# One decoder step of two layers on one core: a 16-column first tile, rotary halves moved by DMA, and a new order of products where each stage opens

## The chip, the cores and the metric

The kernel runs on one core of a Trainium2 chip. The metric is the device time of one execution in microseconds, the median of several runs: 1350.68 us before the change (three runs, 1350.62 to 1351.5). The execution that the profiler took needed 1351.72 us, and its span from first to last instruction is 1349.6 us.

## The reference

Two layers work on 320 tokens of 1024 features: 256 of a new stream (the prompt) and 64 of a running one (the sample, with 256 past positions). A layer is

```
x += 1/2 * post(SwiGLU_1(pre(x)))                          # ffn, 1024 -> 2*2816 -> 1024
x += post(W_out [GLA | DiffAttn+ALiBi | Retention](pre(x)))  # mixer, W_in: 1024 -> 3344
x += 1/2 * post(SwiGLU_2(pre(x)))
```

with `pre` and `post` RMS norms. What the change touches in the mixer is this:

```
a_lr, gq, gk, gv, gr, dq, dk, dv, rq, rk, rv, rg = jnp.split(z, offs, axis=-1)   # a_lr has 16 columns
log_a = jax.nn.log_sigmoid((a_lr @ P['w_gla_a2'][l] + P['b_gla_a'][l]).astype(jnp.float32)) / GLA_TAU
# _rotary, for each head of 64 columns of rq and rk:
return jnp.concatenate([x1 * cos - x2 * sin, x1 * sin + x2 * cos], axis=-1)
# differential attention, two maps per head:
a = p[:, 0] - lam * p[:, 1]
return jnp.einsum('bhqk,bkhv->bqhv', a, vf)
```

Gated linear attention (GLA) and retention are recurrences evaluated in chunks of 64; the attention has four heads with values of 128 columns. Everything is float32.

## The kernel before, in words

Features lie on the 128 partitions and the 320 tokens along the free dimension, so `x[:, k, :]` is the k-th of 8 blocks of 128 features. A weight tile (a "unit") is 1024 rows by 128 columns: 8 blocks of 128 x 128. Each weight and each activation is split in a high part (`w_h`, `xn_h`: rounded to fp32r) and a low part (`w_l`, `xn_l`: the rest), and one block is multiplied with three matmuls, `w_h xn_l`, `w_l xn_h` and `w_h xn_h` (`product`, L678 to L680), so an ordinary tile is 24 matmuls of 320 columns. SP loads raw tiles into six slots (`load`), ScalarE makes `w_h` (`hi`, L537), VectorE makes `w_l` in place (`lo`, L546), TensorE multiplies, and `w_used` gives the slot back to SP. Matmuls with float32 operands (identity, means, masks, scores) are issued as two instructions each.

Six sub-layers follow each other: ffn1, mixer, ffn2, and again. Between two of them TensorE sums the squares of the output (`stat_y`, L719 and L723), ScalarE takes the root, VectorE the reciprocal (L1414), TensorE spreads it over the partitions (`spread`, L731), and VectorE scales y and adds the first block of it to x; GpSimd adds the others (L554). ScalarE then makes `xn_h` (L1095) and VectorE `xn_l` (L1407), block by block. After `spread`, `keep_busy(6)` (L738) multiplies a constant by the identity six times. The first four tiles of a sub-layer are its opening: for block 0 to 3 TensorE waits for `xn_lo` and does the three products of that block for each of the four tiles (`opening_step`), then each tile's blocks 4 to 7 (`opening`). The statistic of the norm (`stat_x`, L713) is put ahead of the fourth tile. The row scale `rs` (L1447) is applied when a tile leaves PSUM. The first opening of all (`first_opening`) is separate: five warming matmuls of 512 columns (`WARM`, L830), transposes of x as it arrives (`turn_x`, L802), then `first_step(k)` (L816, L819, L822) and the statistic; the tiles 4 and 5 follow in `up_pair(0, 2, False)`.

The mixer is written out by hand in `SCHEDULE`, a list that all engines walk in the same order. ("part", v, k0, k1) are products of input tile v; the rest are steps of the three head groups. Each step marks milestones that others wait for (`mark`, `after`). The GLA scores are made in nine levels: ScalarE exponentiates weights, GpSimd multiplies q and k by them (L583), TensorE multiplies (L915), VectorE copies under a mask (L1587, `score`n). Level n+1 waits for `score`n. `rot` is the rotary step: TensorE multiplies z by a signed permutation (L941) and VectorE does PSUM times sin, z times cos, and the sum (L1646, L1647, L1649). The attention goes through 12 pairs of head and query block: `att_s` (scores, L987 to L991), `att_max`, `att_e`, `att_a` (softmax and difference), `att_t` (transposes of the probabilities, L999; for the sample a product with `fold`, L1001, which adds the two maps), a ScalarE copy, `att_o` (times v, L1012). For the sample's block the 128 rows hold the 64 queries of both maps. Then `squares`, `stat`, `root`, `spread` normalise the heads, and `out` 0 to 7 is the opening of the output projection; its tiles 4 to 7 follow (`U_OUT`). While these run, ScalarE and VectorE evict tile v (`y_tile`, `add_square`) and split the weights of unit 6 + v (v below 5).

## Time and profile before

| | |
|---|---|
| median of three runs | 1350.68 us |
| the profiled execution | 1351.72 us, span 1349.6 us |
| TensorE busy (matmul) | 1330.8 us of the span |
| VectorE, ScalarE, GpSimd busy | 821.7, 637.0 and 132.7 us |
| mean granted TensorE clock | 0.997 of full speed |

The instructions of TensorE overlap: one is drawn from its start until its result has left the array, so its length is more than the distance to the next. Distances from start to start, or the pieces of the chain of waits, tell what an instruction costs. Times are microseconds from the start of the span.

### The profile page before, as it was taken

To read this page: it belongs to the slowest core of one execution; us is meant where nothing else is said; L and a number is where in the kernel's file an instruction comes from.
4 is the path that set the end of the run, shared out by engine and by line. 5 is a ranking of instruction groups with operands and counts; after the bars stand their busy time and mean duration, and the time that the engine had idled before them with its cause. 6 is when DMAs were issued, how large, how long until landed. Compare 5 with 4: busy or idle time off the path is not lost.

```text
span 1349.6 us, 24688 instructions
## 1 busy us (share of the span) xinstructions
PE 1330.8 (99%) x9576; PEld 1300.6 (96%) x9576; DVE 821.7 (61%) x1257; ACT 637.0 (47%) x1011; POOL 132.7 (10%) x153
## 2 busy tenths in 40 slices
PE   8999999999999999999999999999999999999998
PEld 7999999998989999999999999999899999999998
DVE  6755543687766855554386555438876677565532
ACT  5444433654466644443464443437435575444333
POOL 1000000550000200000030000005600030000000
PEclk9999999999999999999999999999999999999999
DMA  7555565543344445555544544555333346555552
GB/s 203 170 168 159 161 167 150 157 128 82 96 119 126 124 143 154 147 141 152 152 121 145 155 144 144 152 152 160 96 96 86 98 125 172 146 149 151 145 144 66
DMA packets 351145, 187.16 MB, mean 139 GB/s; under 512 B 6608, under 2 KB 348396, under 8 KB 351080
## 3 DMA queue, kind: packets, MB, share of 16 engines
q1 hardware_dynamic: 347560, 177.37, 46.6%
q0 software_dynamic: 2736, 8.03, 1.8%
q8 instruction: 45, 0.74, 0.2%
q10 hardware_dynamic: 784, 0.86, 0.2%
q14 instruction: 20, 0.16, 0.0%
HBM read 181.90 MB, written 4.33 MB: 138 GB/s over the span
## 4 chain that ended last, share of the span: by engine, by line
PE 92%; DVE 4%; DVEq 1%; issue 1%; ACT 1%; DMA 1%; POOL 0%; ACTq 0%; SPq 0%; POOLq 0%
PE ps L678 28%; PE ps L679 27%; PE ps L680 27%; DVE w_l L546 1%; PE ps L987 1%; PE ps L915 1%; PE ps L738 1%; PE ps L890 1%; PE ps L1012 1%; PE ps L830 1%; PE ps L1025 1%; PE ps L731 0%; PE ps L1001 0%; PE ps L723 0%; DVE tiny L1623 0%
## 5 line engine op out<-in xcount | busy, mean ns | idle before, releaser
L678 PE MATMUL ps<-xn_l,w_h 128*128 128x320 f32 x1808 | 569.7, 315 | 1.2 <-DVE xn_l L1407 0.8
L679 PE MATMUL ps<-xn_h,w_l 128*128 128x320 f32 x1808 | 558.5, 309 | 0.0
L680 PE MATMUL ps<-xn_h,w_h 128*128 128x320 f32 x1808 | 558.4, 309 | 0.0
L546 DVE TENSOR_TENSOR w_l<-raw,w_h 128x1024 fp32r<-128x1024 f32 (+1 forms) x338 | 407.5, 1209 | 167.2 <-ACT w_h L537 166.7
L537 ACT ACTIVATE w_h<-raw 128x1024 fp32r<-128x1024 f32 (+1 forms) x338 | 348.4, 1035 | 216.5 <-DMA raw<-in_ffn_w_down_dram 124.9
L678 PEld LDWEIGHTS ps<-xn_l,w_h 128*128 128x128 f32 x1808 | 339.8, 188 | 6.8 <-DVE xn_l L1407 2.0
L679 PEld LDWEIGHTS ps<-xn_h,w_l 128*128 128x128 f32 x1808 | 339.9, 188 | 1.7
L680 PEld LDWEIGHTS ps<-xn_h,w_h 128*128 128x128 f32 x1808 | 339.7, 188 | 0.0
L678 PE MATMUL ps<-hid_l,w_h 128*128 128x320 f32 x704 | 217.5, 309 | 0.0
L680 PE MATMUL ps<-hid_h,w_h 128*128 128x320 f32 x704 | 217.4, 309 | 0.0
L679 PE MATMUL ps<-hid_h,w_l 128*128 128x320 f32 x704 | 217.4, 309 | 0.0
L679 PEld LDWEIGHTS ps<-hid_h,w_l 128*128 128x128 f32 x704 | 132.2, 188 | 0.0
L680 PEld LDWEIGHTS ps<-hid_h,w_h 128*128 128x128 f32 x704 | 132.2, 188 | 0.0
L678 PEld LDWEIGHTS ps<-hid_l,w_h 128*128 128x128 f32 x704 | 132.2, 188 | 0.0
L1486 DVE TENSOR_TENSOR gate<-ps,rs 128x320 f32<-128x320 f32 x72 | 35.3, 490 | 157.7 <-PE ps L680 157.5
L1153 ACT ACTIVATE gate<-gate 128x320 f32<-128x320 f32 x72 | 34.0, 472 | 146.6 <-DVE gate L1486 146.5
L554 POOL TENSOR_TENSOR x<-x,y 128x320 f32<-128x320 f32 x35 | 36.9, 1087 | 330.2 <-DVE y L1418 330.2
L1157 ACT ACTIVATE hid_h<-up 128x320 f32 (+1 forms) x72 | 34.0, 473 | 70.8 <-DVE up L1492 70.8
L1138 ACT ACTIVATE sq<-ps 128x320 f32<-128x320 f32 x48 | 20.8, 434 | 48.6 <-PE ps L680 48.5
L1492 DVE TENSOR_TENSOR up<-up,gate 128x320 f32<-128x320 f32 x72 | 35.5, 492 | 12.4 <-issue 11.4
L1260 ACT ACTIVATE probs<-probs,tiny 128x128 f32<-128x128 f32 (+2 forms) x40 | 19.3, 482 | 47.9 <-DVE tiny L1623 47.9
L678 PE MATMUL ps<-xw_l,w_h 128*128 128x320 f32 x128 | 40.1, 313 | 0.0
(270 smaller groups left out, 1208.3 us busy)
## 6 DMA issues: line engine op xcount, KB each, us to landing
raw<-in_ffn_w_up_dram SPq DMA_DIRECT2D x172, 512.0 KB, 3.8
raw<-in_ffn_w_down_dram SPq DMA_DIRECT2D x64, 448.0 KB, 3.7
raw<-in_w_in_dram SPq DMA_DIRECT2D x54, 512.0 KB, 3.8
raw<-in_ffn_w_down_dram SPq DMA_DIRECT2D x32, 512.0 KB, 3.9
raw<-in_w_out_dram SPq DMA_DIRECT2D x16, 512.0 KB, 4.1
const<-in_tables_dram POOLq DMA_DIRECT2D x8, 298.0 KB, 4.4
raw<-in_ffn_w_up_dram SPq DMA_DIRECT2D x8, 256.0 KB, 6.4
x_in<-in_x_prompt_dram SPq DMA_DIRECT2D x4, 256.0 KB, 6.2
```

The lines of the kernel that those rows point to most:

```text
L537: act.activation(w_h[s][:, 0:cols], raw[s][:, 0:cols], ACT.Copy).then_inc(w_hi, 1)
L546: dve.tensor_tensor(w_l[s][:, 0:cols], raw[s][:, 0:cols], w_h[s][:, 0:cols], ALU.subtract).then_inc(w_lo, 1)
L554: pool.tensor_tensor(x[:, k, :], x[:, k, :], y[:, k, :], ALU.add).then_inc(x_new, 1)
L678: pe.matmul(out, w_h[s][:, w], xl, start=first, stop=False)
L679: pe.matmul(out, w_l[s][:, w], xh, start=False, stop=False)
L680: return pe.matmul(out, w_h[s][:, w], xh, start=False, stop=last)
L1138: act.activation(sq[b][:, :], ps[:, bank, 0:T], ACT.Square).then_inc(y_sq, 1)
L1153: act.activation(gate[q][:, :], gate[q][:, :], ACT.Silu).then_inc(silu, 1)
L1157: act.activation(tile(hid_h, v), up[q][:, :], ACT.Copy).then_inc(hid_hi, 1)
L1260: i = act.activation(p, p, ACT.Exp, bias=tiny[:, 8 + 2 * s + m:9 + 2 * s + m], accum_out=tiny[:, 12 + 2 * s + m:13 + 2 * s + m])
L1486: dve.tensor_tensor(gate[q][:, :], ps[:, 2 * q, 0:T], rs[:, :], ALU.mult).then_inc(up_mul, 1)
L1492: dve.tensor_tensor(up[q][:, :], up[q][:, :], gate[q][:, :], ALU.mult).then_inc(prod, 1)
```

## The change

In words, in the order of a layer:

- `first_opening`: three warming matmuls of 320 columns where there were five of 512, and the first piece of x_sample comes by SP's queue, ahead of the first weights, not by ScalarE's. The tiles 4 and 5 come into this function: their `w_h xn_h` and `w_h xn_l` products go first, then the wait for `w_lo` and the `w_l xn_h` products; `stat_x` and the transposition of the parameters stand within tile 4. ScalarE makes the high part of unit 4 one step earlier.
- `opening_step`: per block first `w_h xn_h` of four tiles, then `w_l xn_h` of four, and only then the wait for `xn_lo` and `w_h xn_l` of four. It waits for `xn_hi` and for the low parts of all four tiles at its start.
- `spread`: one matmul of 256 constant columns is put ahead of its wait; `keep_busy` makes 4 in place of 6.
- The first tile of the mixer holds 16 columns: its high part lies in columns 0 to 15 of each block and its low part in columns 32 to 47, so that two products per block do for three, and `a2` is loaded twice. Load, `hi` and `lo` of this tile are 16 columns wide.
- `rot` loses its matmul. SP exchanges the halves of rq and rk with eight DMAs per layer (SBUF to SBUF, 32 partitions each), queued among the weight loads behind a wait for `evac`; sin carries the sign. The four VectorE steps move in `SCHEDULE` from before levels 0 and 1 and after levels 2 and 3 to after levels 1, 2, 3 and 4.
- `att_t` of the sample's block is three transposes; `att_o` multiplies 128 columns for it, and VectorE adds the two maps' halves after ScalarE's copy (`att_o`, milestone of DVE), for which `squares` waits.
- While the output tiles run, the weights ahead are split after tiles 3 to 6 (`AHEAD_OUT`), not after tiles 0 to 4 and 6.

```diff
+AHEAD_OUT = {3: (6,), 4: (7, 8), 5: (9, 10), 6: (11,)}
-WARM = 5
+WARM = 3
 SCHEDULE = (
...
-    ... tile_steps(6) + [("past", 0), ("past", 1), ("rot", 0), ("weight", 0)]
-    + P8[7][:1] + [("rot", 1), ("weight", 1)] + P8[7][1:]
+    ... tile_steps(6) + [("past", 0), ("past", 1), ("weight", 0)]
+    + P8[7][:1] + [("weight", 1)] + P8[7][1:]
...
+   ("level", 1), ("rot", 0), ... ("level", 2), ("rot", 1), ... ("level", 3), ("rot", 2), ... ("level", 4), ("rot", 3),
...
+    add("sin", np.sin(ang.astype(np.float32)) * np.where(r % 64 < 32, -1.0, 1.0)[:, None])
 # SP
+                if k == 0:
+                    sp.dma_start(x_in[64:128, 2, 0:2 * P], ins["x_sample"][0, :, 0:2 * P]).then_inc(x_chunk[0], 16)
+                sp.dma_start(low_rank(raw[slot(l, U_MIX)], 0), columns(ins["w_in"], l, slice(0, RANK))
+                             ).then_inc(raw_in[slot(l, U_MIX)], 16)
+                for v in range(1, N_MIX):
...
+                    n = v - RQ - 8
+                    if n in (0, 2):
+                        sp.wait_ge(evac, l * GROUPS + G_MIX + RQ + n + 3)
+                        for g in range(0, P, 32):
+                            sp.dma_start(y[g:g + 32, n:n + 2, :], z[g ^ 32:(g ^ 32) + 32, RQ + n:RQ + n + 2, :]
+                                         ).then_inc(turned_halves[n // 2], 16)
 # TensorE
+            def low_rank_part(s, bank, k0, k1):
+                for k in range(k0, k1):
+                    w = w_h[s][:, k * P:(k + 1) * P]
+                    pe.matmul(ps[:, bank, 0:T], w, xn_l[:, k, :], start=k == 0, stop=False)
+                    mm = pe.matmul(ps[:, bank, 0:T], w, xn_h[:, k, :], start=False, stop=k == KD - 1)
...
             def opening_step(l, u0, n, i, order=range(KD), xh=xn_h, xl=xn_l):
+                pe.wait_ge(w_lo, l * UNITS + u0 + OPENING)
+                pe.wait_ge(xn_hi, (l * 4 + n) * KD + i + 1)
+                for t in range(OPENING):
+                    pe.matmul(out(t), block(w_h, t), xh[:, k, :], start=i == 0, stop=False)
+                for t in range(OPENING):
+                    if u0 + t != U_MIX:
+                        pe.matmul(out(t), block(w_l, t), xh[:, k, :], start=False, stop=False)
                 pe.wait_ge(xn_lo, (l * 4 + n) * KD + i + 1)
                 for t in range(OPENING):
-                    if i == 0:
-                        pe.wait_ge(w_lo, l * UNITS + u0 + t + 1)
-                    tile_part(slot(l, u0 + t), t, i, i + 1, order, xh, xl)
+                    mm = pe.matmul(out(t), block(w_h, t), xl[:, k, :], start=False, stop=i == KD - 1)
...
             def spread(l, m):
+                pe.matmul(ps_rs[:, 0:256], C("ident"), const[:, 0:256], start=True, stop=True)
                 pe.wait_ge(inv_out, l * 3 + m + 1)
...
-                    keep_busy(6)
+                    keep_busy(4)
...
+                for t in range(OPENING, OPENING + 2):      # first_opening
...
+                    part(w_h[t], xn_h, 0, KD, first=True)
+                    part(w_h[t], xn_l, 0, KD)
+                    pe.wait_ge(w_lo, t + 1)
+                    if t == OPENING:
+                        part(w_l[t], xn_h, 0, KD // 2)
+                        pe.wait_ge(first_consts, 16)
+                        stat_x(0, 0)
+                        part(w_l[t], xn_h, KD // 2, KD, last=True).then_inc(w_used, 1)
...
                     for kt in range(KEYS[ATT[n][1]]):      # att_t
-                            mm = pe.matmul(ps[:, 6, kt * P:kt * P + T_S], p, C("fold"), start=True, stop=True)
+                        mm = pe.transpose(ps[:, 6, kt * P:(kt + 1) * P], p, C("ident"))
 # VectorE
+                elif kind == "att_o":
+                    if n % 3 == 2:
+                        after(dve, l, "act", f"att_o{n}")
+                        v = y[:, 2 + n // 3, T_P:T]
+                        mark("dve", dve.tensor_tensor(v, v, ps[:, 7, T:T + T_S], ALU.add), f"att_o{n}")
                 elif kind == "rot":
-                    zt, t = z[:, RQ + n, :], y[:, 7, :]
-                    after(dve, l, "pe", f"rot{n}")
-                    dve.drain()
-                    dve.tensor_tensor(t, ps[:, ROT_BANK[n], 0:T], C("sin"), ALU.mult)
+                    zt, t = z[:, RQ + n, :], y[:, n, :]
+                    dve.wait_ge(turned_halves[n // 2], (l + 1) * 64)
+                    dve.tensor_tensor(t, t, C("sin"), ALU.mult)
                     dve.tensor_tensor(zt, zt, C("cos"), ALU.mult)
```

## Rows read from the trace of the kernel before

**Rows 1.** The page: busy time, share and instructions of each engine.
```profile
PE 1330.8 (99%) x9576; PEld 1300.6 (96%) x9576; DVE 821.7 (61%) x1257; ACT 637.0 (47%) x1011; POOL 132.7 (10%) x153
```

**Rows 2.** Chain of waits: start, length, engine and line, instructions merged.
```profile
280.82 0.54 PE ps L941 x2
...
281.51 0.15 PE ps L679
...
308.48 0.33 PE ps L890 x3
...
351.35 0.61 PE ps L1001 x6
```

**Rows 3.** Timeline, ffn1 to mixer, layer 0: start, length, then idle and releaser.
```profile
250.95 2.76 PE L738 MATMUL ps<-const 128*128 128x256 f32 x12
...
252.25 0.56 ACT L1095 ACTIVATE xn_h<-x,par 128x320 fp32r<-128x320 f32 x1 [0.82 <-DVE x L1424]
...
253.97 0.41 PE L678 MATMUL ps<-xn_l,w_h 128*128 128x320 f32 x1 [0.26 <-DVE xn_l L1407]
```

**Rows 4.** Timeline, mixer to ffn2, layer 0.
```profile
435.21 0.93 PE L731 MATMUL ps<-const,inv 128*128 128x128 f32 x6 [0.47 <-DVE inv L1414]
...
437.38 0.56 ACT L1095 ACTIVATE xn_h<-x,par 128x320 fp32r<-128x320 f32 x1 [2.42 <-DVE x L1424]
...
440.08 0.50 PE L678 MATMUL ps<-xn_l,w_h 128*128 128x320 f32 x1
...
445.74 0.81 DVE L1407 SCALAR_TENSOR_TENSOR xn_l<-x,par,xn_h 128x320 fp32r<-128x320 f32 x1 [0.28 <-ACT xn_h L1095]
```

**Rows 5.** Busy time of stretches; the eighth entry, after POOL, is the granted clock.
```profile
248.70:252.10 3.40, 2.93 (x20) 2.66 (x21) 1.04 (x3) 2.20 (x5) 1.44 (x2) 1.00 0.79 228
...
436.50:439.80 3.30, 3.30 (x9) 2.60 (x8) 3.21 (x7) 1.58 (x4) 2.06 (x3) 0.50 0.03 10
675.40:678.70 3.30, 3.30 (x11) 2.94 (x12) 1.70 (x5) 0.56 (x1) 0.24 (x1) 0.50 0.38 113
```

**Rows 6.** Timeline of the beginning.
```profile
10.23 0.83 PE L816 MATMUL ps<-xn_h,w_h 128*128 128x320 f32 x4 [0.39 <-ACT xn_h L1095]
...
12.04 2.65 SPq L484 DMA_DIRECT2D const<-in_tables_dram  x1
...
28.26 0.78 PE L713 MATMUL ps<-ssum,const 128*128 128x320 f32 x2 [2.06 <-DVE ssum L1442]
```

**Rows 7.** Timeline of VectorE and TensorE: what tile 6 waits for.
```profile
34.33 2.35 DVE L546 TENSOR_TENSOR w_l<-raw,w_h 128x1024 fp32r<-128x1024 f32 x2
...
36.82 0.41 PE L678 MATMUL ps<-xn_l,w_h 128*128 128x320 f32 x1 [0.20 <-DVE w_l L546]
```

**Rows 8.** Line L478 in the window 2.0 to 3.2: x's second piece.
```profile
L478 SPq DMA_DIRECT2D x_in<-in_x_prompt_dram x1: 602/602/602, 2.7 to 2.7; - x1
...
DMA to landing us min/median/max: 6.0/6.0/6.0
```

**Rows 9.** VectorE's groups from 289 to 306.2: busy, mean ns, idle before.
```profile
L1587 DVE COPY_PREDICATED probs<-mask,ps 128x384 f32<-128x384 uint8 x3 | 1.8, 587 | 2.1 <-PE ps L915 1.7 <-issue 0.2 <-PE ps L890 0.2
L1649 DVE TENSOR_TENSOR z<-z,y 128x320 f32<-128x320 f32 x2 | 1.7, 851 | 0.1
L1647 DVE TENSOR_TENSOR z<-z,const 128x320 f32<-128x320 f32 x2 | 1.3, 648 | 0.0
L1646 DVE TENSOR_TENSOR y<-ps,const 128x320 f32<-128x320 f32 x2 | 1.0, 492 | 0.2
```

**Rows 10.** Timeline of the levels, of both engines.
```profile
305.38 0.70 PE L915 MATMUL ps<-sq 32*64 32x64 f32 x40 [0.99 <-DVE probs L1587]
...
306.23 0.58 DVE L1587 COPY_PREDICATED probs<-mask,ps 128x384 f32<-128x384 uint8 x1 [1.00 <-PE ps L915]
```

**Rows 11.** Timeline of TensorE, end of the heads and of the output tiles.
```profile
404.47 0.83 PE L1029 MATMUL ps<-const,z 128*128 128x1 f32 x6 [0.35 <-ACT z L1283]
...
433.24 0.74 PEld L719 LDWEIGHTS ps<-const,ssum 128*128 128x128 f32 x6 [0.30 <-DVE ssum L1478]
```

More of the change, by code:

```diff
@@ L164, in milestones @@
                 act.append(f"att_o{n}")
+                dve.append(f"att_o{n}")
         elif kind == "squares":
@@ L204, in constants @@
     add("head128", np.ones((P, 1)) / 128.0)
-    rot = np.zeros((P, P))
-    for g in (0, 64):
-        for i in range(32):
-            rot[g + 32 + i, g + i] = -1.0
-            rot[g + i, g + 32 + i] = 1.0
-    add("rot", rot)
     pos = np.concatenate([np.arange(T_P), PAST + np.arange(T_S)]).astype(np.float32)
@@ L215, in constants @@
     add("cos", np.cos(ang.astype(np.float32)))
-    add("sin", np.sin(ang.astype(np.float32)))
+    add("sin", np.sin(ang.astype(np.float32)) * np.where(r % 64 < 32, -1.0, 1.0)[:, None])
     lg = np.log(1.0 - 2.0 ** (-5.0 - np.arange(H)))
@@ L274, in build @@
         NCONST = sum(n for _, n in table_at.values())
-        FIRST = table_at["rot"][0]
+        FIRST = table_at["cos"][0]
         N_PAR = 16 * 9
@@ L394, in build @@
         masks_loaded = sem("masks_loaded")
+        turned_halves = [sem(f"rotary_halves_exchanged{n}") for n in range(2)]
         par_mm = sem("par_mm")
@@ L829, in first_opening @@
                 for _ in range(WARM):
-                    pe.matmul(ps[:, 3, :], sq_2[:, 0:P], sq_2[:, P:P + 512], start=True, stop=True)
+                    pe.matmul(ps[:, 3, 0:T], sq[0][:, 0:P], sq[0], start=True, stop=True)
                 pe.wait_ge(pads_set, 2)
@@ L841, in first_opening, with part @@
                         turn_x(k + 3)
-                pe.wait_ge(first_consts, 16)
-                stat_x(0, 0)
-                pe.wait_ge(par_loaded, N_PAR)
-                pe.transpose(ps_m[:, 3, 0:ROWS], par_in[0:ROWS, :], C("ident")[0:ROWS, 0:ROWS]).then_inc(par_mm, 1)
+                for t in range(OPENING, OPENING + 2):
+                    def part(w, v, k0, k1, first=False, last=False):
+                        for k in range(k0, k1):
+                            mm = pe.matmul(ps[:, t, 0:T], w[:, k * P:(k + 1) * P], v[:, k, :], start=first and k == 0,
+                                           stop=last and k == KD - 1)
+                        return mm
+                    pe.wait_ge(w_hi, t + 1)
+                    part(w_h[t], xn_h, 0, KD, first=True)
[6 more added lines that the diff above has]
+                        part(w_l[t], xn_h, KD // 2, KD, last=True).then_inc(w_used, 1)
+                        pe.wait_ge(par_loaded, N_PAR)
+                        pe.transpose(ps_m[:, 3, 0:ROWS], par_in[0:ROWS, :], C("ident")[0:ROWS, 0:ROWS]).then_inc(par_mm, 1)
+                    else:
+                        part(w_l[t], xn_h, 0, KD, last=True).then_inc(w_used, 1)
             half_rows = lambda h: slice(64 * (h % 2), 64 * (h % 2) + 64)
@@ L933, in mixer_step @@
                     mark("pe", heads_out(5 + n, n, scores, gv_tok, s0_a, q_s[:, :]), f"gla_o{n}")
-                elif kind == "rot":
-                    pe.wait_ge(evac, l * GROUPS + G_MIX + RQ + n + 2)
-                    if n >= 2:
-                        shared_free(l, kind, n)
-                    else:
-                        after(pe, l, "act", "abs")
-                        after(pe, l, "dve", "minus")
-                    mark("pe", pe.matmul(ps[:, ROT_BANK[n], 0:T], C("rot"), z[:, RQ + n, :], start=True, stop=True), f"rot{n}")
                 elif kind == "ret_s":
@@ L1071, in _ @@
                 spread(l, 1)
-                keep_busy(6)
+                keep_busy(4)
                 ffn(l, U_F2, G_F2, 4, 3, 2)
@@ L1082, in _ @@
             act.dma_start(par_in[0:DEPTH * KD, :], ins["ffn1_norm_pre"].rearrange("l (k p) -> (l k) p", p=P)).then_inc(gain_loaded, 16)
-            for c in range(KD // 2):
+            for c in range(1, KD // 2):
                 cols = slice(2 * c * P, 2 * (c + 1) * P)
@@ L1124, in pre @@
                     split_hi(l, n, k, x, norm)
+                    if l == 0 and n == 0 and k == KD - 1:
+                        hi(act, l, u0 + 4)
                     if k:
@@ L1127, in pre @@
                 square(KD - 1)
-                for v in (4, 5):
+                for v in (5,) if l == 0 and n == 0 else (4, 5):
                     hi(act, l, u0 + v)
```

80 lines of the change are left out of this document (45 added, 35 removed).

## The prediction

> **What bounds the kernel now.** I read the page first: TensorE is busy for 1330.8 of 1349.6 us [rows 1]. Nothing near 10% can be had without taking matmuls away, and nearly every matmul that goes is time. But VectorE, at 821.7 us, is not far behind on average, and in some stretches it decides; so I went to the chain of waits for the price of one matmul, and to the timelines of the places that the diff touches for what is late there. In the chain a product of 320 columns takes 0.15 us (0.1465 over long stretches), a float32 matmul of 320 columns such as `rot` 0.54 for its two instructions, the three `fold` matmuls 0.61, three transposes 0.33 [rows 2]. The timelines show TensorE idle, or occupied with constants, at three kinds of place: each passage between sub-layers [rows 3, 4], the beginning [rows 6, 7], and VectorE's chain in the GLA levels [rows 10].
>
> The profiled execution took 1351.72 us, 1.04 above the median. I work out a difference against it and take it from the median, 1350.68.
>
> **Passages (five).** In ffn1 to mixer, `keep_busy` fills 250.95 to 253.71 and the first product starts at 253.97, released by `xn_lo`. `xn_hi` of block 0 is there at 252.25 + 0.56 = 252.81 [rows 3]. After the change four constant matmuls, 2.76 x 4/6 = 1.84, end at 252.79, and products start at 252.8: 1.1 us earlier. The eight products that need no `xn_lo` take 1.17, about what it still lacks. The matmul added to `spread` stands in the wait for the reciprocal, 0.47 us by the idle time of L731 [rows 4]; for 256 columns it takes 0.54 x 256/320 = 0.43 [rows 2]. So it costs nothing while that wait covers it, and at half the clock at most 0.43.
>
> From the mixer to ffn2 the same step was worse: `keep_busy` ran at clock 0.50 [rows 5], so products started only at 440.08, while `xn_hi` was there at 437.94 [rows 4]. The granted clock fell to its lower level (1.2 GHz) in two stretches, here and at 675.4, while after ffn1 of layer 0, where less of the stretch was idle, it stayed at 1.00 (2.4 GHz) [rows 5]. The filler in `spread` adds work exactly there; I take it that the clock holds. Then products start at 437.95, 2.1 us earlier. The next limit is `xn_lo` of block 7, at 446.55 [rows 4]: tile 0 needs it after 4 x 12 + 9 products (8.35 us), at 446.3, so almost nothing is lost. In the mixer's passages it is lost a little sooner, because the first tile has fewer products. Sum outside the mixer's own start: 2.1 + 2.1 (the one at 675) + 1.1 (mixer to ffn2 of layer 1, as in rows 3) = 5.3. If the clock falls all the same, each of the first two gives 1.4 less: lower bound 2.5.
>
> **The mixer, per layer.** TensorE loses 1.1 at the passage, 8 products of the first tile (1.17; most of it swallowed by the wait for `xn_lo` of block 7), and four `rot` matmuls, 4 x 0.54 = 2.16 [rows 2]. If TensorE decided alone, that would be 3.3 to 4.4. It doesn't. Level n+1 waits for `score`n, VectorE does the rotary steps between them, and TensorE stands idle for 0.99 at level 5 already [rows 10]. Before, two of four rotary steps were over when the levels began; now all four lie between score 1 and score 5. One costs 0.49 + 0.65 + 0.85 = 2.0 us, so two more are 4.0. The product with sin read PSUM; now both its inputs are in SBUF, like those of the other two products, which take 0.65 and 0.85 where L1646 takes 0.49 [rows 9]: 0.16 to 0.36 more each, about 1.0 for four. VectorE's spare time in this stretch is 2.1 and the 1.00 ahead of score 5 [rows 9, 10], 3.1. It starts earlier by what TensorE gained until level 1, 1.1 + 2 x 0.54 = 2.2. What arrives at level 5 and 6 is 2.2 + 3.1 - 4.0 - 1.0 = 0.3. So I cost the rotary part at a gain of 0.3 per layer, the passage and the narrow tile included. Bounds: 3.3 if VectorE's waits give way, -1.0 if the four steps cost 2.3 each and the spare time can't be used.
>
> The Trainium skill speaks to this too (SBUF — State Buffer, "SBUF: two separate sides"): a VectorE operation with two SBUF inputs and a GpSimd operation that reads SBUF lock each other out for a whole instruction. By that rule the sin product can wait out a GpSimd multiplication; the trace agrees for the two products that it could concern, and by the rule in full the gain of 0.3 would be a loss.
>
> The eight rotary DMAs stand in SP's queue. They wait for tile 6's and tile 8's eviction, well before the next weight load is due (a tile is 24 products, 3.5 us). An issue took between 0.6 [rows 8] and 2.65 us [rows 6]; I take 0.6, the form being plain, so four fit and nothing is late. The narrow tile makes load, `hi` and `lo` shorter; nobody waits for them, so 0.
>
> Fold: 0.61 becomes 0.33 four times a layer [rows 2], 1.1. The trace has no `att_o` of the sample's block at 128 columns. From below it costs what it did, from above its six instructions take 6 x 0.54/2 x 128/320 = 0.65 where six of 64 columns take 0.61, as the fold's [rows 2]; I take the upper end, 0.04 x 4 lost. The last block adds VectorE's addition ahead of `squares` c, for which TensorE already stands 0.35 [rows 11]: between 0.1 and 0.5, I take 0.3. Net 0.6.
>
> Output tiles: TensorE (its weight load) waits 0.30 for VectorE's last addition of squares, behind a weight split of 1.2 [rows 11, 7]; with the split put behind it, 0.2 is gained. The splits of tiles 6 and 7 come later, but TensorE works on tiles 4 and 5 for 7 us; if that cover failed, each would cost up to 1 us.
>
> Per layer 0.3 + 0.6 + 0.2 = 1.1, two layers 2.2, with bounds of -0.4 and 8.2.
>
> **The beginning.** TensorE idles 2.06 before `stat_x` [rows 6], and now tile 4 starts there. But tile 6 waits for its low part, which ended at 36.68, not for TensorE [rows 7], and VectorE makes that only after `rs`, which hangs on `stat_x`. That statistic now comes 20 products, 2.93 us, after the opening's last, where it came 2.2 after (the idle 2.06 and the last product's 0.15): 0.7 later. The start itself: `turn_x(2)` stands ahead of the first step and needs x's second piece, which landed at 2.65 + 6.0 = 8.6 [rows 8], now issued some 0.6 later. The first step thus comes at 9.0 to 9.6, not at 10.23 [rows 6]: 0.6 to 1.2 gained. Together -0.1 to 0.5 gained, and with a lower clock, for TensorE has less to do before 9 us, about 1.5 lost. I take 0.
>
> **Sum.** 5.3 + 2.2 + 0 = 7.5: 1344.2 for the profiled execution, 1343.2 for the median.
>
> **Rivals.**
> A. *TensorE decides everywhere.* Each removed matmul is time, the rotary steps fit. For it: 1330.8 us of TensorE [rows 1]. Against it: 0.99 idle at level 5 [rows 10]. Per layer 3.3 instead of 0.3: 6.0 more, 1337.2.
> B. *The clock falls more often.* Shorter warming, four constants for six, and a first stretch in which only three transposes per block run. For it: two of five passages fell already [rows 5]. Against it: the filler. It costs 1.5 at the beginning and 1.4 at two passages: 1347.5. The Trainium skill (TensorE: Matmul & The Clock Gate, Part 4) says that transposes don't count as busy for the clock as other matmuls do; no row here tests it. By it this rival is likelier at the beginning, where transposes take the place of the warming.
> C. *Slower.* The SP queue holds the weights back: if each rotary issue takes 2.65 us [rows 6], four take 10.6, 7.1 beyond the tile that covers them, and ScalarE, which walks one list, stands at the weight's high part with the level weights behind it. Four such groups are up to 28 us: 1371. It turns the forecast's gain into a loss from (7.5/4 + 3.5)/4 = 1.3 us per issue on.
> D. *The rotary steps wait for their DMAs or lock with GpSimd,* each 0.5 dearer: 4.0 lost, 1347.2.
>
> **How the numbers follow.** Forecast 0.46 (own range 1341 to 1345), A 0.23, B 0.14, D 0.11, C 0.04, and 0.02 for a loss from some other new wait. The range 1337.3 to 1347.6 holds the first four but for their tails. Within 0.2% (2.7 us, about what a measurement can tell from no change) begins at 1348: the tails of B and D, 0.04. Slower is C and the other loss, 0.06, and faster 0.90.
>
> **What would show it.** No `fold` or `rot` in TensorE's groups; the first product of a passage right after `xn_hi` and `keep_busy`; clock 1.00 at the passages; a wait of TensorE on L1587 at levels 4 to 7 of 1 to 3 us a layer, where A has none; L713 of the beginning near 28; SP's rotary issues at 0.6. I am wrong if TensorE's waits in the levels are below 0.5 (A), or if ScalarE waits for a weight right after the rotary DMAs (C).

## The result, and the profile after

The changed kernel takes 1355.16 us (median of 13 runs, 1349.92 to 1357.66) where the kernel before takes 1350.6 beside it: ratio 1.0033, 95% interval 1.0026 to 1.004. It is slower, by 4.6 us or 0.33%; I had forecast 1343.2. The profiled execution is itself one of 1355.16 us, with a span of 1353.4. Over the 13 runs the time goes largely with the mean granted clock: the fastest, 1349.92, had 0.998, the four slowest (1355.98 to 1357.66) 0.992 or 0.993.

The page's row of busy times answers to [rows 1]: TensorE lost 8.2 us of work, and the span grew by 3.8.

```profile
PE 1322.6 (98%) x9506; PEld 1294.2 (96%) x9506; DVE 822.2 (61%) x1265; ACT 636.9 (47%) x1011; POOL 135.9 (10%) x153
```

Where the time went can be read from the starts of the same TensorE instructions in both traces. In the table, a positive number is time lost against the kernel before within that stretch. The third column is the changed kernel with the old beginning (the first experiment), where only the rest of the change acts.

| stretch (start before, us) | forecast | changed | old beginning |
|---|---|---|---|
| start to first `spread` (250.18) | 0 | +5.05 | +0.35 |
| layer 0, first `spread` to level 8 (315.11) | -0.3 | -0.15 | +0.13 |
| layer 0, level 8 to `spread` after the output tiles (435.21) | -0.8 | +1.74 | +1.45 |
| layer 0 mixer to ffn2, and ffn2 (673.12) | -2.1 | -1.33 | -1.88 |
| ffn2 to ffn1 of layer 1 (675.28 to 913.16) | -2.1 | -1.84 | -1.86 |
| layer 1, first `spread` (915.26) to level 8 | -0.3 | +0.23 | 0.00 |
| layer 1, level 8 to `spread` (1100.11) | -0.8 | +0.74 | +0.79 |
| layer 1 mixer to ffn2, and ffn2 (1339.49) | -1.1 | -0.72 | -0.73 |

(Stretches leave out the wait for the reciprocal in ffn passages, which differs by up to 0.11. The +0.23 holds a fall of the clock at 970.2.) Three things failed: the beginning, the part from the heads to the last output tile, and a little of the passages. The beginning alone turns the sign.

**Beginning.** The timeline of TensorE, then of VectorE; columns are start, length, engine and line, then idle time and releaser. The last two rows are the end of tile 5 and the start of tile 6, which started at 36.82 before [rows 7].

```profile
5.83 0.55 PE L844 MATMUL ps<-const,x_in 128*128 128x128 f32 x3
9.50 0.90 PE L844 MATMUL ps<-const,x_in 128*128 128x128 f32 x3 [3.12 <-DMA x_in<-in_x_prompt_dram]
10.05 1.41 PE L858 MATMUL ps<-xn_h,w_h 128*128 128x320 f32 x4
...
30.81 0.70 PE L754 MATMUL ps<-ssum,const 128*128 128x320 f32 x2
...
34.39 1.34 PE L887 MATMUL ps<-xn_h,w_l 128*128 128x320 f32 x8
39.30 0.63 PE L697 MATMUL ps<-xn_l,w_h 128*128 128x320 f32 x1 [3.57 <-DVE w_l L565]
```
```profile
32.02 2.15 DVE L1492 RECIPROCAL rs<-sq 128x320 f32<-128x320 f32 x1 [0.86 <-ACT sq L1145]
...
36.81 2.35 DVE L565 TENSOR_TENSOR w_l<-raw,w_h 128x1024 fp32r<-128x1024 f32 x2
```

The first step starts at 10.05 (before: 10.23), but four products take 1.41 where they took 0.83 [rows 6], and the last product of the eight steps starts 1.84 late (27.73 against 25.89). `stat_x` is 2.55 late (30.81 against 28.26): 1.84 by those steps, the other 0.71 because it now stands behind 20 products. `rs` and the low part of tile 6 hang on it, and tile 6 starts 2.48 late. TensorE, which had done the tiles 4 and 5 by then, stands idle for 3.57 ahead of it. The remaining 2.57 are lost between there and the first `spread`. The view of the granted clock (the last figure but two in each row) shows a slow stretch for each half of the loss:

```profile
0.00:7.60 7.60, 4.43 (x13) 2.60 (x13) 2.30 (x5) 1.28 (x1) 1.41 (x6) 1.00 0.59 175
7.60:14.40 6.80, 4.90 (x20) 4.86 (x21) 2.83 (x6) 4.46 (x9) 0.00 (x0) 0.50 1.11 348
14.40:38.30 23.90, 21.33 (x147) 20.87 (x145) 20.19 (x37) 14.45 (x23) 3.43 (x3) 1.00 0.63 165
38.30:45.20 6.90, 5.90 (x22) 5.91 (x23) 5.64 (x11) 3.74 (x7) 0.00 (x0) 0.51 0.29 69
441.10:444.50 3.40, 3.40 (x13) 2.88 (x13) 1.21 (x4) 0.17 (x1) 0.00 (x0) 0.50 0.31 92
675.40:678.80 3.40, 3.40 (x26) 3.40 (x26) 1.18 (x1) 2.25 (x2) 0.00 (x0) 1.00 0.56 167
970.20:973.60 3.40, 3.40 (x15) 3.40 (x14) 3.20 (x4) 0.00 (x0) 1.68 (x1) 0.50 0.07 17
```

Twice, 6.8 to 6.9 us at 1.2 GHz. The first time TensorE had done no more than a few transposes in the 3.0 us since its warming ended, the second time it had been idle for 2.6. The drop that [rows 5] show at 675.4 is gone; the one at 436.5 has moved to 441.1.

**Levels.** TensorE waits for VectorE at three levels of layer 0, the levels 3, 4 and 5 (one before, 0.99 [rows 10]); in layer 1 it waits twice, 1.14 and 1.54. VectorE's groups from 289 to 311.5 give the price of a rotary step, 0.83 + 0.62 + 0.80 = 2.25.

```profile
301.00 0.70 PE L972 MATMUL ps<-sq 32*64 32x64 f32 x40 [0.98 <-DVE probs L1632]
...
305.63 0.70 PE L972 MATMUL ps<-qk 32*64 32x64 f32 x40 [1.53 <-DVE probs L1632]
...
310.28 0.70 PE L972 MATMUL ps<-sq 32*64 32x64 f32 x40 [1.22 <-DVE probs L1632]
```
```profile
L1695 DVE TENSOR_TENSOR y<-y,const 128x320 f32<-128x320 f32 x4 | 3.3, 827 | 0.0
L1698 DVE TENSOR_TENSOR z<-z,y 128x320 f32<-128x320 f32 x4 | 3.2, 797 | 0.3
L1696 DVE TENSOR_TENSOR z<-z,const 128x320 f32<-128x320 f32 x4 | 2.5, 615 | 0.0
```

**Output tiles.** The first step of output tile 0, TensorE's timeline: it stands 1.10 for VectorE's low parts, a wait the kernel before did not have. The statistic of the last heads waits 0.61 (before: 0.35 [rows 11]). `stat_y` starts 1.04 later than the usual distance from one product to the next; before it was 0.20. From start to start the pieces are: level 8 to the statistic of the first heads 83.31 (before 83.89), from there to output tile 0 2.78 (1.77), to the statistic of the last heads 3.95 (3.69), to `stat_y` 29.56 (28.78). In layer 1 the first three are the same within 0.03, and the fourth is as before (28.58 against 28.56).

```profile
404.50 0.49 PE L1047 MATMUL ps<-const,probs 128*128 128x128 f32 x3
406.10 0.83 PE L726 MATMUL ps<-xw_h,w_h 128*128 128x320 f32 x4 [1.10 <-DVE w_l L565]
...
410.05 0.83 PE L1074 MATMUL ps<-const,z 128*128 128x1 f32 x6 [0.61 <-ACT z L1330]
...
439.61 0.83 PE L760 MATMUL ps<-const,ssum 128*128 128x1 f32 x6 [0.87 <-DVE ssum L1523]
```

**Passages.** ffn1 to mixer, layer 0, answers to [rows 3]: `keep_busy` is 1.89 long, not 2.76, and the first product follows it directly.

```profile
255.99 1.89 PE L780 MATMUL ps<-const 128*128 128x256 f32 x8
258.01 0.83 PE L726 MATMUL ps<-xn_h,w_h 128*128 128x320 f32 x4
```

### The profile page after: what moved, and what is told of

It reads as the page before. It is cut to its first block, busy times and chain, and to the rows that moved or that the text cites. A ratio compares the mean times of both kernels' runs of the same rounds, so it can differ in the third digit from the quotient of the medians.

```text
span 1353.4 us, 24588 instructions
## 1 busy us (share of the span) xinstructions
PE 1322.6 (98%) x9506; PEld 1294.2 (96%) x9506; DVE 822.2 (61%) x1265; ACT 636.9 (47%) x1011; POOL 135.9 (10%) x153
## 4 chain that ended last, share of the span: by engine, by line
PE 89%; DVE 5%; POOL 2%; DMA 1%; DVEq 1%; issue 1%; ACT 1%; SPq 0%; ACTq 0%; POOLq 0%
PE ps L697 26%; PE ps L699 26%; PE ps L698 26%; POOL x L573 2%; DVE w_l L565 1%; PE ps L726 1%; PE ps L732 1%; PE ps L729 1%; DMA raw<-in_ffn_w_up_dram 1%; PE ps L948 1%; PE ps L972 1%; PE ps L1036 1%; PE ps L1070 1%; PE ps L1057 0%; DMA x_in<-in_x_prompt_dram 0%
## 5 line engine op out<-in xcount | busy, mean ns | idle before, releaser
L697 PE MATMUL ps<-xn_l,w_h 128*128 128x320 f32 x1704 | 537.3, 315 | 3.6 <-DVE w_l L565 3.6
L698 PE MATMUL ps<-xn_h,w_l 128*128 128x320 f32 x1704 | 528.0, 310 | 0.0
L699 PE MATMUL ps<-xn_h,w_h 128*128 128x320 f32 x1704 | 527.9, 310 | 0.0
L697 PEld LDWEIGHTS ps<-xn_l,w_h 128*128 128x128 f32 x1704 | 321.7, 189 | 7.7 <-issue 4.8
L698 PEld LDWEIGHTS ps<-xn_h,w_l 128*128 128x128 f32 x1704 | 321.8, 189 | 1.0
L699 PEld LDWEIGHTS ps<-xn_h,w_h 128*128 128x128 f32 x1704 | 321.7, 189 | 0.0
L1140 ACT ACTIVATE xn_h<-x,par 128x320 fp32r<-128x320 f32 x48 | 27.0, 563 | 25.1 <-DVE x L1469 11.2
```

The costliest lines, as they stand in the source:

```text
L697: pe.matmul(out, w_h[s][:, w], xl, start=first, stop=False)
L698: pe.matmul(out, w_l[s][:, w], xh, start=False, stop=False)
L699: return pe.matmul(out, w_h[s][:, w], xh, start=False, stop=last)
L1140: act.activation(dst[:, k, :], src[:, k, :], ACT.Copy, scale=scale).then_inc(xn_hi, 1)
```

## The experiments

Theory: the beginning costs about 5, by a low clock in the first steps and by `stat_x` behind 20 products. The rest gains only 1 to 2, for the rotary steps lie in VectorE's level chain and the first output tile waits for four low parts at once. Main rival: the beginning is no cause, and time comes back elsewhere as the clock moves. Each kernel was timed with 11 runs unless said. Times of the kernel before beside them: 1350.5 to 1350.6. The edits are given in short.

### The old beginning

```diff
-WARM = 3   (320 columns)      +WARM = 5   (512 columns)
-x_sample piece 0 by SP        +all four pieces by ACT
-tiles 4, 5 around stat_x      +stat_x, then up_pair(0, 2)
```

> The changed kernel with the beginning of the kernel before: five warming matmuls of 512 columns, all four pieces of x_sample issued by ACT, tiles 4 and 5 of the first FFN by up_pair behind stat_x, hi(4) behind the squares. Everything else is as changed. Theory 'the beginning': the first spread of the changed kernel starts 5.05 us later than before (255.22 against 250.18), the rest of the change is worth -1.3 in all (the end is +3.7), so this kernel ends 5 under the changed one: 1350 (1348.5 to 1351.5), first spread at 250.2, tile 6 at 36.8. Rival 'the clock moves elsewhere': a beginning without its extra half-speed windows lets one fall at a later passage (spread of the mixer, 435 or 1100), and only 1.5 to 3.5 of the 5 come back: 1352 to 1353.5. Rival 'something behind the beginning': the first spread was late for another reason, the time stays within 1 of 1355.

Measured: 1350.04 (1349.42 to 1352.01), ratio 0.9997, interval 0.9988 to 1.0006. That is 5.1 under the changed kernel, and the first `spread` is at 250.53. The theory holds: without the new beginning the kernel is as fast as the one before, and the rest of the change brings nothing that the time can show. Of the 5.5 us between the two profiled executions 4.7 lie ahead of the first `spread`; the other 0.8 lie behind it, mostly where the clock of the changed kernel fell, at 441.1 and 970.2, and this one's did not. So a part of the rival stands: the clock falls at different places (here at 28.9 and 302.0), and whether the beginning has to do with the later falls is not shown.

### Its three parts, each undone alone on the changed kernel

```diff
 e5_warm:  +WARM = 5, 512 columns
 e6_tiles: +stat_x behind the eight steps, tiles 4, 5 by up_pair
 e9_x:     +x_sample piece 0 by ACT
```

> The changed kernel with one part undone: the five warming matmuls of 512 columns instead of three of 320. The old beginning as a whole gave back 5.1. Theory 'warming': in the changed kernel the clock is at 0.50 from 7.6 to 14.4, over the first step and a half, which puts stat_x 2.5 later (30.8 against 28.3), and all that follows (rs, the low parts of tile 6, the idle 3.9 ahead of tile 6, the second window at half clock from 38.3) comes from that: with the old warming the first step runs at 1.00, the second window goes, and the time is 1350 to 1351, -4 to -5. Rival 'order of tiles 4 and 5': the idle time ahead of tile 6 comes from stat_x standing behind 20 products: the old warming then gives back only the 2 of the first window, 1353. Rival 'the piece of x': turn_x(2) still waits for the x piece that lands at 9.45, behind a warming that ends near 8; only 1 comes back.

> The changed kernel with one part undone: tiles 4 and 5 of the first FFN by up_pair behind stat_x, stat_x right behind the eight first steps, hi(4) behind the squares. Warming and the order of the x pieces stay as changed. Theory 'order of tiles 4 and 5': stat_x comes 20 products (2.9 us) earlier, rs and the low parts of tile 6 with it; TensorE has tiles 4 and 5 (7 us) to cover them, the idle 3.9 ahead of tile 6 falls to some 1 and the second window at half clock goes: first spread 3 to 3.5 earlier, 1351.5 to 1352. Rival 'warming': the order of tiles 4 and 5 is what it saves, not what it costs, and the time stays at 1355 or rises by up to 1, the idle time then standing ahead of stat_x (2.06 in the kernel before).

> The changed kernel with one part undone: all four pieces of x_sample are issued by ACT, none by SP between the first x piece and the first weights. Theory 'SP late': in the changed kernel the first raw weights land at 7.82 against 6.03 and the second x piece at 9.45, and turn_x(2) stands 3.12 for it; with one issue less ahead of them on SP (0.6 to 0.7 each) these land some 1 earlier, the first step starts 1 to 2 earlier (8 to 9), still at half clock: 1353 to 1354, and if TensorE's idle stretch shrinks enough for the clock to stay up, 1351. Rival 'ACT late instead': the sample piece is late on ACT and turn_x(0) waits for it; no gain, within 0.7 of 1355.

Measured: warming 1351.63 (1351.12 to 1354.2), tiles 1351.55 (1350.11 to 1353.81), piece of x 1352.98 (1350.11 to 1355.14). The three sum to 9.3 where all together gave 5.1. One reason is that they share a loss. The other is the clock behind the beginning: in the profiled executions the three are at the first `spread` only 2.5, 2.6 and 1.1 ahead of the changed kernel, and the other 0.7 to 1.1 of each lies behind it, where none of the three profiles has the falls at 441.1 and 970.2. Views of the granted clock and the waits show how the loss is shared. With the old warming the eight steps run at full clock and take 15.69 from the first product to the last (before 15.66, changed 17.68). The idle time ahead of tile 6 stays all the same, and a slow stretch follows it:

```profile
7.60:14.40 6.80, 6.42 (x40) 5.24 (x39) 4.92 (x11) 4.50 (x11) 0.00 (x0) 1.00 1.09 344
38.00:41.40 3.40, 3.40 (x13) 3.40 (x14) 2.81 (x5) 1.89 (x3) 0.00 (x0) 0.50 0.20 50
```
```profile
37.94 0.58 PE L697 MATMUL ps<-xn_l,w_h 128*128 128x320 f32 x1 [3.56 <-DVE w_l L565]
```

With the old order of tiles 4 and 5 the first steps stay slow (their first four products take 1.42), but the wait of 3.57 at tile 6 is gone, against the old idle 2.07 ahead of `stat_x`. Tile 6 starts no earlier for it (39.47 against 39.30); what is saved is the slow stretch behind it, for the only slow stretch behind `stat_x` (30.9 to 34.3) falls on the tiles 4 and 5:

```profile
29.74 0.78 PE L754 MATMUL ps<-ssum,const 128*128 128x320 f32 x2 [2.07 <-DVE ssum L1469]
30.79 0.55 PE L697 MATMUL ps<-xn_l,w_h 128*128 128x320 f32 x1 [0.17 <-DVE w_l L565]
```

Without SP's extra issue the wait for x's piece is 1.92, not 3.12, but the first step starts only 0.37 earlier (9.68) and stays at 0.50. `stat_x` (30.94) and tile 6 start no earlier than in the changed kernel:

```profile
39.42 0.63 PE L695 MATMUL ps<-xn_l,w_h 128*128 128x320 f32 x1 [3.56 <-DVE w_l L563]
```

The 1.1 at its first `spread` is a second slow stretch half as long in this profile (39.1 to 42.5); that the piece of x is the cause is not shown. So my theory on the warming was too strong (3.5, not 4 to 5): the idle time of 3.57 is there at full clock too and comes from the order of the tiles alone. Filling 2.06 of idle time opened one of 3.57, which costs as much as the warming does.

### Rotary halves by the constant matmul again

```diff
-("level", 1), ("rot", 0) ... ("level", 4), ("rot", 3)
+("past", 1), ("rot", 0) ... ("rot", 1), ("weight", 1) ... ("level", 2), ("rot", 2) ... ("level", 3), ("rot", 3)
-dve.wait_ge(turned_halves[n // 2], (l + 1) * 64)
+after(dve, l, "pe", f"rot{n}")
```

> As the kernel with the old beginning, and the rotary halves come from the constant matmul again, at the four old places of SCHEDULE (two before level 0, two behind levels 2 and 3), with no exchange by DMA. Theory 'DVE pays for the rotary': with the exchange the levels gave back 1.8 in layer 0 and 2.2 in layer 1 while the two matmuls removed before level 0 gained 1.05 and 1.08, so the matmul form is 0.7 to 1.1 faster per layer, 1.5 to 2 in all: 1348 to 1348.5 if the old beginning alone gives 1350; TensorE starts levels 4 to 8 without the waits of 1.1 to 1.7 us on L1587. Rival 'TensorE pays': four 384-column matmuls less are 4 x 0.54 per layer of TensorE's time, so the matmul form is 1 to 2 slower per layer (+2 to +4 against the old beginning alone). Rival 'no matter': the level waits come from other edits (AHEAD_OUT, low-rank tile), within 0.5.

Measured: 1349.26 (1347.3 to 1349.99), 0.8 under the old beginning alone, with intervals that overlap. The traces say it more sharply. Counted from the first `spread` of each layer, against the kernel before, the exchange is 1.5 and 1.1 ahead of the matmul form at level 0, loses 2.07 and 1.95 from level 2 to level 8, where the matmul form loses nothing, and is 0.54 and 0.89 behind it there. (The clock fell at 302 in the kernel with the exchange; in the changed kernel, where it did not, the 2.07 are 1.79. The expectation calls the matmuls 384 columns wide; they have 320.)

### The low parts of the output tiles waited for later

```diff
-pe.wait_ge(w_lo, l * UNITS + u0 + OPENING)
+pe.wait_ge(w_hi, l * UNITS + u0 + OPENING)
 pe.wait_ge(xn_hi, ...)
 for t in range(OPENING): w_h * xh
+pe.wait_ge(w_lo, l * UNITS + u0 + OPENING)
 for t in range(OPENING): w_l * xh
```

> As the kernel with the old beginning, and opening_step waits for the high parts of its four tiles ahead of the first products and for the low parts only behind the four w_h x xh products. Theory 'output tiles wait for all low parts': the first step of the output tiles stood for 1.10 in layer 0 and 1.29 in layer 1 on w_l of all four tiles; it now starts about 1 earlier in each, and what is late next is the squares of the third group of heads (0.61): 1.0 to 2.2 less than the old beginning alone, 1348 to 1349. Rival 'the low parts are late anyway': the wait only moves four products (about 0.7 us) down, and the gain is 0.7 per layer less what the following wait takes, under 0.5 in all. The same edit touches the opening tiles of the FFN and of the mixer, where the low parts are already there: no change there.

Measured: 1348.55 (1347.84 to 1351.99), 1.5 under the old beginning alone, with intervals that overlap; the traces give 0.86 and 0.90 from level 8 to the output tiles' end in the two layers. The wait of 1.10 shrinks to 0.28, behind four products (TensorE's timeline):

```profile
400.63 0.85 PE L724 MATMUL ps<-xw_h,w_h 128*128 128x320 f32 x4
401.76 0.86 PE L728 MATMUL ps<-xw_h,w_l 128*128 128x320 f32 x4 [0.28 <-DVE w_l L563]
```

The theory holds in size and place: a loop over four tiles that had waited tile by tile now waited for the last of four.

### The old places of the weight splits

```diff
-AHEAD_OUT = {3: (6,), 4: (7, 8), 5: (9, 10), 6: (11,)}
+AHEAD_OUT = {0: (6,), 1: (7,), 2: (8,), 3: (9,), 4: (10,), 6: (11,)}
```

> As the kernel with the old beginning, and AHEAD_OUT spreads the high splits of output tiles 6 to 11 as before (one per evicted tile, from tile 0 on). Theory 'late splits': in the changed kernel stat_y of the mixer stood 0.7 to 1.0 in layer 0 behind an ACT that waited for the raw weights (1.67 and 0.70 idle at 433.08 and 436.65); with the old places the last output tiles start 0.5 to 1 earlier in layer 0 and not at all in layer 1: 0.5 to 1 less, 1349 to 1349.5. Rival 'the places don't matter': the raw weights land when they land, and ACT waits there in either order, within 0.3 of the old beginning alone. Rival 'the change was right': splits at tiles 0 to 2 delay the evictions of those tiles, 0.3 to 1 slower.

Measured: 1351.57 (1350.76 to 1353.46), 1.5 slower. My theory fell: the later splits are no loss. With the old places `stat_y` of layer 0 starts 1.65 later than a product's usual distance, with the new ones 1.01; in layer 1 0.68 against 0.14. Part of the 1.5 is the clock, which fell at 438 and 1066 in the profiled run: the piece around 1066 took 1.55 more.

### Rotary steps late, and early

Both on the kernel with the old beginning and the later wait (1348.55).

```diff
 e8_rotlate:   +("level", 5), ("rot", 0) ... ("level", 8), ("rot", 3)
 e10_rotearly: +P8[7][:1], ("rot", 0) ... ("part", 8, 0, 5), ("rot", 1) ... level 2, rot 2 ... level 3, rot 3
```

> As the kernel with the old beginning and the later wait for low parts (1348.55), and the four rotary steps with their exchange by DMA stand behind levels 5, 6, 7 and 8 in SCHEDULE, not behind 1 to 4. In the kernel with the old beginning TensorE stood at levels 3 to 5 of layer 0 for 1.14 and 1.70 on VectorE, whose step behind level 1 took 1.85 + 1.00 + 1.71 beside GpSimd at 290.8 to 295.4 and 0.48 x 3 once GpSimd was idle. Theory 'place, not exchange': behind level 5 GpSimd is idle and VectorE has 2.5 us of gaps; the levels keep 1 to 1.6 of the 2.07 they gave back in layer 0 and about 1 of 0.9 to 1 in layer 1: 1346 to 1347. Rival 'VectorE is full either way': 4 x 1.45 us more between level 5 and ret_dec make the retention decays late, ret_kt waits 2 to 3 per layer: 1348 to 1351. Rival 'no matter': within 0.5 of 1348.5.

> As the kernel with the old beginning and the later wait for low parts (1348.55), with the exchange by DMA and the rotary steps nearly where the matmul form has them: 0 and 1 ahead of level 0 (behind tile 7's first half and tile 8's first part), 2 and 3 behind levels 2 and 3. The first exchange lands at 283.6, so step 0 can run from there. VectorE is idle 1.7 + 1.1 us between 282 and 288.3, and a step takes 1.45 alone and up to 4.6 beside GpSimd. With the steps behind levels 5 to 8 levels 3 to 5 kept their gain (-3.8 at level 5) but gave back 2.4 by level 8 and 1.5 more by the heads. Theory 'place': two steps in the idle time ahead of level 0 cost level 0 at most 1, and the levels give back at most 1 in place of 2.07: 1347 to 1348. Rival 'VectorE has a fixed sum of work from 276 to 317': whatever the place, levels plus heads come out within 0.5 of 1348.5. Rival 'beside GpSimd it is dearest': two steps of 3 to 4.6 us there make tile 7's and 8's evictions late, TensorE stands 2 ahead of level 0: 1350 to 1352.

Measured: late 1348.25 (1347.61 to 1349.37), early 1356.33 (5 runs, 1353.79 to 1356.95). Late, levels 3 to 5 kept what was won (level 5 at -3.81 against the kernel before), then levels 7 and 8 gave back 2.4 and the stretch from there to the heads, where `ret_kt` needs VectorE's decays, 1.7. What is left is 0.3 in the time, less than these runs can tell from nothing: the work is VectorE's, wherever it stands. Early, it stands for the exchange itself. VectorE's timeline of that kernel:

```profile
281.12 1.23 DVE L563 TENSOR_TENSOR w_l<-raw,w_h 128x1024 fp32r<-128x1024 f32 x1
285.40 0.82 DVE L1676 TENSOR_TENSOR y<-y,const 128x320 f32<-128x320 f32 x1 [3.05 <-DMA y<-z]
286.14 1.02 DVE L1677 TENSOR_TENSOR z<-z,const 128x320 f32<-128x320 f32 x1
287.24 1.72 DVE L1679 TENSOR_TENSOR z<-z,y 128x320 f32<-128x320 f32 x1
```

TensorE then stands 3.44 ahead of level 1. I had expected the exchange to have landed at 283.6, when its last DMA had been issued; here a DMA of it lands 2.0 to 2.6 after its issue. The only idle time that VectorE has ends before the halves are there; that is what the matmul form could use.

### Without the filler in `spread`

```diff
-pe.matmul(ps_rs[:, 0:256], C("ident"), const[:, 0:256], start=True, stop=True)
```

> As the kernel with the old beginning (1350.04), without the one 256-column product that spread makes ahead of its wait for inv. Theory 'the filler holds the clock': the kernel before fell to 0.50 at 436.4 and 675.4, in two of the five passages; the changed kernel with the old beginning held 1.00 at all of them. Without the filler the clock falls again at one or two passages, 1.7 us each: 1351.5 to 1353. Rival 'the order of the products fills the passage': opening_step now begins with four products of high parts while the low part of x is made; TensorE's idle time in the passage is shorter by that and not by the filler: within 0.5 of 1350. Rival 'the filler is in the way': 0.1 each of five passages, 1349.5.

Measured: 1351.39 (1349.81 to 1352.53), 1.35 above the old beginning alone, with intervals that overlap. The clock falls at both passages again, where with the filler the same windows show 1.00:

```profile
437.30:440.70 3.40, 3.40 (x12) 2.95 (x12) 2.10 (x5) 0.56 (x1) 0.64 (x1) 0.50 0.08 24
676.20:679.60 3.40, 3.40 (x11) 3.04 (x12) 1.63 (x4) 0.56 (x1) 0.17 (x1) 0.51 0.38 110
```
```profile
437.30:440.70 3.40, 3.20 (x19) 2.68 (x20) 2.49 (x5) 0.69 (x2) 1.03 (x2) 1.00 0.09 28
675.40:678.80 3.40, 3.28 (x19) 2.72 (x19) 2.30 (x5) 0.56 (x1) 0.84 (x2) 1.00 0.37 110
```

It doesn't hold it always: of twelve profiled kernels with the filler the clock fell near 436 to 441 in four, near 675 in none; of two without it (this one and the kernel before), in both at both places.

### The fold matmuls back

```diff
-pe.transpose(..., C("ident")) for the sample's block, 128 columns, VectorE adds the halves
+pe.matmul(..., C("fold")), 64 columns, no addition
```

> As the kernel with the old beginning and the later wait for low parts (1348.55), with the constant fold matmuls of the attention heads back (and the narrow eviction, and no addition on VectorE behind every third head). I forecast 0.6 per mixer for their removal; the traces show 0.24 between level 8 and the statistic of the heads in each mixer, and 0.26 lost again at the statistic of the last heads, which waits for ACT's squares behind VectorE's addition (0.78 against 0.52 before). Theory 'a wash': back with the fold, within 0.4 of 1348.5. Rival 'forecast right, hidden elsewhere': the removal gives 0.6 per mixer, 1349.8. Rival 'the addition costs more': without it the time is 0.5 to 1 lower, 1347.6 to 1348.

Measured: 1348.55 (1347.4 to 1349.91), the same. A wash in the time, but not in the traces. From level 8 to the statistic of the first heads it takes 83.91 in both layers, where every kernel with the transposes but the one with the late rotary steps takes 83.30 to 83.57: the transposes gain about 0.6 a layer there, not the 0.24 that I wrote ahead of the run. VectorE's addition takes 0.26 back, for with the fold the statistic of the last heads waits 0.35 again:

```profile
405.16 0.83 PE L1061 MATMUL ps<-const,z 128*128 128x1 f32 x6 [0.35 <-ACT z L1315]
```

That leaves some 0.33 a layer for the transposes, 0.7 in all, which is within what the times of two such kernels differ by chance.

### What has shown a gain, together

```diff
 old beginning, rotary by matmul, later wait for the low parts; passages, filler, AHEAD_OUT and transposes as changed
```

> The kernel with the old beginning, the rotary halves by the constant matmul at the old places (1349.26 with that alone), and the wait for the low parts behind the first products (1348.55 with that alone). If the two add up: 1350.04 - 0.8 - 1.5 = 1347.75 (1347 to 1348.3). Rival 'one hides the other': the passage that each shortens ends in the same wait (squares of the third group of heads) and only one counts, 1348.5. It is also the kernel that keeps of the change only what has shown a gain: passages, high parts first, the transposes in place of the fold.

Measured: 1346.69 (1345.98 to 1348.6), ratio 0.9975, interval 0.9966 to 0.9984. It beats both kernels: 3.8 under the one before, beside which it ran, and 8.5 under the changed one's median. The rotary matmuls were worth 1.9 here and 0.8 without the later wait; the ranges overlap, so the difference of the two is not shown.

Three parts of the change were never undone alone: the narrow first tile, the order of products within `opening_step`, and four constants for six.

## Why the prediction was wrong

- **The beginning, forecast 0, was +5.05.** This is the step that failed most, and it failed in three places. First, my own terms did not give 0: at most 0.5 gained against 1.5 lost by the clock is a loss of 1.0 to 1.6. Second, the gain by an earlier start was 0.18, not 0.6 to 1.2, and the low clock cost 2.02 in the eight steps, not 1.5; with the 0.71 of the statistic, which I had right as 0.7, that makes `stat_x` 2.55 and tile 6 2.48 late. Third, I put the idle time ahead of tile 6 at nothing. I had written that tile 6 hangs on `rs` and not on TensorE, and so had the idle time (3.57) before me, but not what follows it: a second stretch at half clock, 6.9 us long, for another 2.57. The experiments part the two: with the old warming the steps are at full speed and the idle time stays (3.56), with the old order of tiles it goes.
- **Rival B** named this mechanism ("less to do before 9 us") and priced it at 1.5 there, a third of what it was; it did not have the second stretch. The clock at 0.50 from 7.6 on stands behind a stretch with a few transposes in it. By the Trainium skill (TensorE: Matmul & The Clock Gate, Part 4) transposes don't count as busy in the same way. That agrees, but TensorE was also idle there, and no run here parts the two.
- **Rotary, passage into the mixer and narrow tile, forecast 0.3 a layer,** was 0.15 gained in layer 0 and 0.23 lost in layer 1, the latter with a fall of the clock; the other profiles with this form and place, where they have no fall there, show between 0.17 gained and 0.09 lost. The mechanism was right: four steps in the level chain, at 2.25 on average where I had 2.0 + 0.25. That the average fits is in part luck: the first step took 4.56 beside GpSimd, the other three 1.46 each. The waits of TensorE at the levels (3.7 in layer 0, 2.7 in layer 1) are about the 1 to 3 that I named, at the levels 3 to 5 where I had 4 to 7. Rival A, TensorE decides, fell. (Its 1337.2 lies just outside the range that was to hold it.)
- **Rule on the shared side of SBUF.** The step at 290.81 in the kernel with the old beginning took 1.85 + 1.00 + 1.71, the next one, from 296.06, 0.48 + 0.49 + 0.49; GpSimd's 1.81 and 1.82 us multiplications stood beside the first alone:

```profile
290.81 1.85 DVE L1675 TENSOR_TENSOR y<-y,const 128x320 f32<-128x320 f32 x1
292.60 1.00 DVE L1676 TENSOR_TENSOR z<-z,const 128x320 f32<-128x320 f32 x1
293.67 1.71 DVE L1678 TENSOR_TENSOR z<-z,y 128x320 f32<-128x320 f32 x1
...
296.06 0.48 DVE L1675 TENSOR_TENSOR y<-y,const 128x320 f32<-128x320 f32 x1
```
```profile
290.51 1.81 POOL L600 TENSOR_TENSOR sq<-z,ssum 128x640 f32<-128x640 f32 x1
292.40 0.85 POOL L591 TENSOR_TENSOR ssum<-decay 128x320 f32<-128x320 f32 x1
293.21 1.82 POOL L600 TENSOR_TENSOR qk<-z,wgt 128x640 f32<-128x640 f32 x1
```

  By the Trainium skill (SBUF — State Buffer, "SBUF: two separate sides") the two engines lock each other out for whole instructions; the trace agrees in these rows, and the average of a step stayed near my figure because three of the four in that kernel fell outside. Rival D, each 0.5 dearer, did not come: the average is 2.25.
- **Heads and output tiles, forecast -0.8 a layer, were +1.7 and +0.7.** The fold came out in kind: 0.58 gained ahead of the statistics, where I had 0.96, and 0.26 lost to VectorE's addition, where I had 0.3. And I had not seen one wait at all: the new `opening_step` asks for the low parts of all four output tiles, 1.10 in layer 0 and 1.13 in layer 1, where the old one asked tile by tile; it put output tile 0 1.0 later in each layer. The diff shows it; my prediction looked only at which operations fell away, not at what the moved wait stood for. The gain of 0.2 at `stat_y` turned into 0.8 lost in layer 0, behind a ScalarE that waited 1.67 for raw weights; the places of the splits are not the reason, for the old places made it worse, and the cause stays open.
- **Passages, forecast 5.3 outside the mixers, gave 3.9,** 4.5 with the old beginning. The term was the right one. That the filler would hold the clock was thinly founded: in the stretch of [rows 5] that kept the clock TensorE was idle for 0.47, in stretches as long ahead of the two falls for 0.51 and 0.60. Two passages fell short most: mixer to ffn2 in layer 0, where the clock fell at 441.1 all the same, and in layer 1, at 0.72 for 1.1.
- **Rival C** (SP's queue) fell: the sixteen issues took 0.51 to 0.63 each.

The sum of the errors: 5.05 at the beginning, 4.8 in the mixers, 1.4 at the passages, 11.2 together, which is the end at +3.7 for a forecast of -7.5. Why 1346.69 of the best kernel is still 3.5 above the forecast, I did not part.

## What to carry to other kernels

Work that waits on a chain of another engine is not brought forward by filling the idle time ahead of it: ask what the filled work pushes back, and whether the idle time reappears one step later, larger, with a fall of the clock behind it. When a loop is regrouped so that like products stand together, its wait becomes the wait for the last of the group; put each wait directly ahead of the first product that reads the data. A matmul that moves data is cheap where VectorE's chain decides, even if TensorE bounds the kernel as a whole: count the engine that decides in that very stretch. And when the terms of a sum are on paper, take their sum, not a round figure near it.

## What was unexpected of the hardware

- Stretches at the low clock lasted 6.8 and 6.9 us in the changed kernel's beginning, 3.4 at every passage. In the kernel before, with five matmuls of 512 columns ahead, the clock stayed at 1.00 from 6.35 to 436.4. In six of the nine variants with that old beginning it fell at 28.6 to 29.6, behind the 2.07 idle ahead of `stat_x`, and it cost next to nothing: the first `spread` came 0.20 to 0.66 later than in the kernel before, in the three without the fall 0.16 to 0.54.
- The changed kernel's runs spread over 7.7 us (1349.92 to 1357.66), those of the kernel before over 3.4. Profiled runs of its variants show drops of the clock at different places (28.9, 302, 304, 436, 970), each of 3.4 us, which costs 1.7 where TensorE is the bound; differences under that are safer read from the traces, stretch by stretch.
- In the changed kernel an exchange of 32-partition blocks of 80 KB from SBUF to SBUF landed 2.2 to 3.7 us after its issue, four issues taking 2.4 to 2.5; the matmul that it replaced takes 0.54.
